# Convolution taps inside the first projection, per-token norm sums, and a tail shared with GpSimd

## The reference, cut to what matters

```python
def conformer_conv(h, w_pw1, b_pw1, w_dw, b_dw, ln_g, ln_b, w_pw2, b_pw2):
    u = h @ w_pw1 + b_pw1                      # 512x1024 @ 1024x2048
    a, gate = jnp.split(u, 2, axis=-1)
    u = a * jax.nn.sigmoid(gate)
    u = lax.conv_general_dilated(              # causal, depthwise, 31 taps
        u, w_dw[:, None, :], window_strides=(1,), padding=[(CONV_WIDTH - 1, 0)],
        dimension_numbers=("NWC", "WIO", "NWC"), feature_group_count=CONV_CHANNELS) + b_dw
    u = jax.nn.silu(layernorm(u, ln_g, ln_b))  # mean and variance over the 1024 channels
    return u @ w_pw2 + b_pw2

def dilated_group(q, k, v, bias_table, window, dilation): ...
    bias = jnp.transpose(bias_table[t5_bucket(dist * dilation)], (2, 0, 1))   # a diagonal of the table per head
    logits = jnp.einsum("bnidhc,bnjdhc->bndhij", qb, kk) * (HEAD_DIM ** -0.5) + bias

def second_block(x, ...):
    ...
    h = h + rms_norm(mixed, mix_norm_post[l])  # MIX_POST in the kernel
    hn = rms_norm(h, ffn_norm_pre[l])          # FFN_PRE
    ...
    return h + rms_norm(ffn, ffn_norm_post[l]) # FFN_POST
```

## Time and profile before

| what | value |
|---|---|
| median of three runs | 1901.59 us |
| the profiled execution's own time | 1901.71 us |
| its span | 1899.9 us |
| mean granted PE clock | 0.971 |
| PE, DVE, ACT, POOL busy | 93%, 57%, 35%, 12% of the span |
| share of the chain that ended last: PE, DVE, ACT | 77%, 17%, 3% |

### The profile page before, as it was taken

How to read it: one execution, slowest core, us unless ns; L and a number is a source line. 1 busy time by engine, 2 the same in 40 slices (tenths; PEclk the granted TensorE clock), 3 DMA queues, 4 the chain that set the end, 5 groups by cost and what they waited for, 6 DMA issues and landing times.

```text
span 1899.9 us, 20795 instructions
## 1 busy us (share of the span) xinstructions
PE 1775.3 (93%) x7977; PEld 1394.9 (73%) x7977; DVE 1088.5 (57%) x1277; ACT 666.1 (35%) x951; POOL 222.3 (12%) x136
## 2 busy tenths in 40 slices
PE   6969699999999999999999999989899699999996
PEld 5747388888888878778888888756456478888884
DVE  6999755442444555664424444568646777626754
ACT  4234343221223244332212234555443344314431
POOL 2013210000000200010000013661200300000001
PEclk9979899999999999999999999989998899999998
DMA  4212012331232311122312322422201112322221
GB/s 178 87 44 73 1 67 89 115 117 67 88 120 91 118 67 56 68 102 107 121 67 91 116 92 100 144 73 80 68 37 67 66 67 88 124 87 88 97 92 44
DMA packets 29151, 164.54 MB, mean 87 GB/s; under 512 B 4347, under 2 KB 7035, under 8 KB 12700
## 3 DMA queue, kind: packets, MB, share of 16 engines
q1 hardware_dynamic: 24800, 158.11, 23.6%
q10 hardware_dynamic: 4284, 5.53, 0.9%
HBM read 153.92 MB, written 4.46 MB: 83 GB/s over the span
## 4 chain that ended last, share of the span: by engine, by line
PE 77%; DVE 17%; ACT 3%; issue 2%; POOL 1%; DMA 0%; ACTq 0%; DVEq 0%; SPq 0%; POOLq 0%
PE PS L592 24%; PE PS L594 24%; PE PS L593 24%; DVE CV L1662 3%; DVE T_hid L1662 3%; DVE W_lo L1632 2%; DVE R L1617 1%; DVE H_lo L1612 1%; ACT W_hi L1036 1%; DVE X L2186 1%; DVE SSUM L2075 1%; PE PS L934 1%; PE PS L886 1%; DVE CV L1675 1%; POOL ISC L1583 1%
## 5 line engine op out<-in xcount | busy, mean ns | idle before, releaser
L592 PE MATMUL PS<-H_hi,W_hi 128*128 128x512 f32 x1600 | 645.6, 403 | 42.7 <-DVE W_lo L1632 22.2
L593 PE MATMUL PS<-H_lo,W_hi 128*128 128x512 f32 x1600 | 628.7, 393 | 0.0
L594 PE MATMUL PS<-H_hi,W_lo 128*128 128x512 f32 x1600 | 628.7, 393 | 0.0
L1036 ACT ACTIVATE W_hi<-W_raw 128x2048 fp32r<-128x2048 f32 (+2 forms) x132 | 266.6, 2020 | 761.6 <-PE PS L594 761.5
L592 PEld LDWEIGHTS PS<-H_hi,W_hi 128*128 128x128 f32 x1600 | 303.8, 190 | 131.1 <-issue 56.7
L1632 DVE TENSOR_TENSOR W_lo<-W_raw,W_hi 128x2048 fp32r<-128x2048 f32 (+2 forms) x132 | 335.6, 2542 | 45.4 <-ACT W_hi L1036 45.1
L594 PEld LDWEIGHTS PS<-H_hi,W_lo 128*128 128x128 f32 x1600 | 303.6, 190 | 65.1
L593 PEld LDWEIGHTS PS<-H_lo,W_hi 128*128 128x128 f32 x1600 | 304.1, 190 | 60.3 <-issue 1.9
L592 PE MATMUL PS<-HID_hi,W_hi 128*128 128x512 f32 x640 | 250.7, 392 | 10.0 <-DVE HID_lo L1738 9.9
L1499 POOL TENSOR_TENSOR SSUM<-SSUM,SQ 128x512 f32<-128x512 f32 x52 | 93.6, 1799 | 1378.4 <-ACT SQ L1069 1375.8
L593 PE MATMUL PS<-HID_lo,W_hi 128*128 128x512 f32 x640 | 250.0, 391 | 0.0
(11 more groups left out here) (263 smaller groups left out, 1460.2 us busy)
## 6 DMA issues: line engine op xcount, KB each, us to landing
W_raw<-in_inp SPq DMA_DIRECT2D x13, 1024.0 KB, 4.8
W_raw<-in_pw SPq DMA_DIRECT2D x12, 1024.0 KB, 4.8
W_raw<-in_gu0a SPq DMA_DIRECT2D x11, 1024.0 KB, 4.7
W_raw<-in_gu0b SPq DMA_DIRECT2D x11, 1024.0 KB, 4.8
W_raw<-in_gu1a SPq DMA_DIRECT2D x11, 1024.0 KB, 4.8
W_raw<-in_gu1b SPq DMA_DIRECT2D x11, 1024.0 KB, 4.7
W_raw<-in_gu2a SPq DMA_DIRECT2D x11, 1024.0 KB, 4.7
W_raw<-in_gu2b SPq DMA_DIRECT2D x11, 1024.0 KB, 4.8
```

The costliest lines, as they stand in the source:

```text
L592: nc.tensor.matmul(dst[:], wh, x_hi[:, k, :], start=(k == first), stop=False)
L593: nc.tensor.matmul(dst[:], wh, x_lo[:, k, :], start=False, stop=False)
L594: return nc.tensor.matmul(dst[:], wl, x_hi[:, k, :], start=False, stop=(k == last))
L1036: nc.scalar.activation(W_hi[b][:, 0:n], W_raw[b][:, 0:n], ACT.Copy).then_inc(w_hi, 1)
```

## The change

- **Taps inside pw1.** PE does 105 taps (tiles 1 and 3 whole, tile 5 from tap 7, tile 7 from tap 12). One tap's three products (L703 to L705 of the new code) follow each k-tile's three from pw1's unit 3 on: 80 taps there and 25 behind. DVE does 143 taps. ACT makes all the diagonals, hi and lo, twelve of 128x128 for each chunk of six taps, in three buffers. POOL makes none.
- **Bias table.** Three products after the last tap, one per group of four heads, leave 4x384 values in PSUM. ACT copies them to fvec, now 4x3x384 and in the memory of H_hi. Three DMAs, each read from four partitions with a broadcast of 128, write the same bias_scratch. ACT waits for all three ahead of the first feed-forward's first H_hi; DVE's wait is gone.
- **LayerNorm.** The sums of squares are column products (one column of ones; one token per partition, 128x4 in all). The root and the reciprocal are of 128x4. Four products with a broadcast and the identity spread the result back over a PSUM bank (`token_spread`). Two small activations load ACT's tables early. The last weight split of pw1 on DVE stands behind the mean's subtractions.
- **MIX_POST, FFN_POST.** The same column sums (`token_sum`) and spreads. ACT's squares stand ahead of its weight splits, and the last unit's splits (ACT's and DVE's) stand behind the root and behind the first two tiles.
- **Tail.** For FFN_POST, DVE does tiles 0 to 4 and writes its temporary to PSUM. ACT scales Y of tiles 5 to 7 and copies R, and POOL multiplies and adds. The output DMAs are issued in another order.
- In pw1's unit 0 ACT's root for the first norm stands ahead of the weight split.

```diff
+PE_TILES = [(1, 0), (3, 0), (5, 7), (7, 12)]
+DVE_TILES = [(0, 31), (2, 31), (4, 31), (5, 7), (6, 31), (7, 12)]
+DVE_TAPS = [5, 8, 21, 24, 24, 24, 24]
+CHUNK = 6
+FIRST_TAP = 48
...
+            def token_sum(n):
...
+                    for b in range(4):
+                        last = nc.tensor.matmul(AUX[0][:, b:b + 1], tokens(src, b), ones[:, 0:1],
+                                                start=(part == 0 and b == 0), stop=(part == 2 and b == 3))
+            def token_spread(bank, made):
+                for b in range(4):
+                    last = nc.tensor.matmul(tokens(bank, b), R4[:, b:b + 1].to_broadcast([P, P]), ident, start=True, stop=True)
...
-                    nc.tensor.matmul(AUX[1 + h % 2][:, 0:DIAG], table_wide[:, h, :], onehot[:, h // GROUP_HEADS, :],
-                                     start=True, stop=True).then_inc(fvec_ps, 1)
+                for g in range(3):
+                    nc.tensor.matmul(PS[1 + g][0:GROUP_HEADS, 0:DIAG], table[:, GROUP_HEADS * g:GROUP_HEADS * (g + 1)],
+                                     onehot[:, g, :], start=True, stop=True).then_inc(fvec_ps, 1)
...
+                        last = product(j % 2, L.kt, half, k, H_hi, H_lo)
...
+                        n = SLOTS * j + 8 * half + k - FIRST_TAP
+                        if n >= 0:
+                            conv_tap(n)
...
+                if n == FFN0 and m.i is None and m.c == 0:
+                    act.wait_ge(scr_out, 48)
...
-            act.dma_start(bias_scratch.rearrange("h p d -> p h d"), fvec[:]).then_inc(scr_out, 16)
+            for g in range(3):
+                act.dma_start(bias_scratch[GROUP_HEADS * g:GROUP_HEADS * (g + 1)],
+                              fvec[:, g, :].unsqueeze(1).to_broadcast([GROUP_HEADS, P, DIAG])).then_inc(scr_out, 16)
...
-            dve.wait_ge(scr_out, 16)
...
+            for n in range(POOL_LAST):
+                m = DT - POOL_LAST + n
+                pool.wait_ge(y_scaled, n + 1)
+                nc.gpsimd.tensor_tensor(Y[:, m, :], Y[:, m, :], R[:], ALU.mult).then_inc(t_pool, 1)
+                pool.wait_ge(t_pool, n + 1)
+                nc.gpsimd.tensor_tensor(X[:, m, :], X[:, m, :], Y[:, m, :], ALU.add).then_inc(x_pool, 1)
```

More of the change, by code:

```diff
@@ L275, in build @@
         CVacc = T_hid
[L277 to L281, removed]
+        UP_hi = sb("UP_hi", [P, 2, PADDED], F32R, at=arena + 17408)
+        UP_lo = sb("UP_lo", [P, 2, PADDED], F32R, at=arena + 21760)
+        D_hi = [sb(f"D_hi{i}", [P, CHUNK, P], F32R, at=w_at + 11264 * i + 8192) for i in range(3)]
+        D_lo = [sb(f"D_lo{i}", [P, CHUNK, P], F32R, at=w_at + 11264 * (3 + i) + 8192) for i in range(3)]
         tap_hi = sb("tap_hi", [P, CONV_WIDTH * DT], F32R, at=arena + 68352)
@@ L663, in _ @@
[L663 to L688, removed]
-            last = nc.tensor.matmul(AUX[3][:], ones, CV[:, CONV_DVE - 1, :], start=False, stop=True)
-            last.then_inc(ln_sum_ready, 1)
+                pe.wait_ge(tab_in, 32)
@@ new lines, in _ @@
+            L = layers["pw1"]
+            unit(L, At(0), H_hi, H_lo, after(h_lo_made, 0))
+            rms_sum(0)
+            for j in range(1, L.n):
+                pe.wait_ge(w_lo, j + 1)
+                if j >= 2:
+                    pe.wait_ge(acc_free, j - 1)
+                for half in range(2):
+                    for k in range(L.kt):
+                        last = product(j % 2, L.kt, half, k, H_hi, H_lo)
+                        if k == L.kt - 1:
+                            last.then_inc(acc_ready, 1)
+                        n = SLOTS * j + 8 * half + k - FIRST_TAP
+                        if n >= 0:
+                            conv_tap(n)
@@ L1140, in _ @@
-            steps(act, L.n, glu_step, first=1, last=2)
-            conv_hi(2)
-            act.wait_ge(fvec_made, 12)
-            act.dma_start(bias_scratch.rearrange("h p d -> p h d"), fvec[:]).then_inc(scr_out, 16)
-            for n, (m, t0, t1) in enumerate(CONV_CHUNKS):
-                if n:
-                    diagonal_hi(n)
-                if n == 0:
-                    split_hi(act, L, At(L.n - 1))
-                if t0 and m > CONV_DVE:
-                    take_conv(m - 1)
-            take_conv(DT - 1)
+                nc.scalar.activation(UP_hi[:, p % 2, 0:n], U[:, m, 0:n], ACT.Copy).then_inc(u_hi, 1)
@@ new lines, in diagonals @@
+            def diagonals(c):
+                if c == 0:
+                    act.wait_ge(w_parts, 2)
+                if c >= 3:
+                    act.wait_ge(conv_pe, CHUNK * (c - 2))
+                for x, (m, t) in enumerate(PE_TAPS[CHUNK * c:CHUNK * (c + 1)]):
+                    for dst, tap in ((D_hi, tap_hi), (D_lo, tap_lo)):
+                        w = tap[:, t * DT + m:t * DT + m + 1].bitcast(F32)
+                        last = nc.scalar.activation(dst[c % 3][:, x, :], ident, ACT.Copy, scale=w)
+                last.then_inc(diag_made, 1)
@@ new lines, in take_bias, with warm_table @@
+            def take_bias(g):
+                act.wait_ge(fvec_ps, g + 1)
+                nc.scalar.activation(fvec[:, g, :], PS[1 + g][0:GROUP_HEADS, 0:DIAG], ACT.Copy).then_inc(fvec_made, 1)
+            def warm_table(function, n):
+                if n:
+                    act.wait_ge(warmed, n)
+                nc.scalar.activation(warm[:, 0:1], epst[:], function).then_inc(warmed, 1)
+            for g in range(SLOTS, SLOTS * L.n):
+                beside_pw1(g)
+            glu_gate(L.n - 1)
@@ L1643, in _ @@
             HALO = CONV_WIDTH - 1
-            todo = [(m, t) for m in range(CONV_DVE) for t in range(CONV_WIDTH if m < CONV_DVE - 1 else CONV_SPLIT)]
+            todo = [(m, t) for m, end in DVE_TILES for t in range(end)]
+            taken_steps = [0]
             def conv(count, upto):
```

350 lines of the change are left out of this document (210 added, 140 removed).

## The result

The changed kernel takes 1926.99 us (median of 4 runs, 1924.4 to 1928.94), the kernel before 1901.24 in the same comparison: a ratio of 1.0132, 95% interval 1.0115 to 1.0150. It is slower by 25.7 us where I forecast 8.5.

The account below looks back on a forecast made before the run. PE was taken to bound most of the time, with taps' and LayerNorm's gains hidden beneath the table's DMA. Sum: 1901.7 + 19.0 (DMA stall) - 7.2 (MIX_POST) - 3.3 (tail) = 1910.2 us; range 1853 to 1917.

Parts of the forecast that it names:

- Taps: pw1 and convolution: last tap ends at 179.4, last join at 182.1, 29.7 us earlier; DVE barely keeps up.
- Rate of the table's DMA: Bias table: one partition group yields 29 GB/s, so the DMAs take 83 us and land at 270; chance 0.72.
- My two engines at 141 ns a packet: Bias table: two engines serve a partition group, each 2048-byte packet taking 141 ns, giving 29 GB/s.
- Who waits: Feed-forward's start: ACT's first H_hi waits for the table until 270, making the layer 19.0 us later than before.
- Everywhere else PE is the bound, and the change leaves that alone: Outside the changed places: PE bounds the time and nothing moves; no term in the sum.
- no rival: DMA no bound: 1858.1, chance 0.20 (0.17 near 1858); late taps beside the stall: up to 1917.7, chance 0.05.
- LayerNorm: From last join to first scaling: 14.2 us instead of 17.5, scaling at 196.3; the gain lies beneath the DMA.
- my 8.5 us for subtracting and squaring with PE cold: Part of LayerNorm's 14.2 us: subtracting and squaring, with the table load ahead and PE cold, take 8.5.
- MIX_POST: Norm after the mixer: R ready 9.4 us earlier, 7.2 net of DVE's deferred split; bounds 5 and 9.4.
- the deferred split of 2.29 us: MIX_POST: DVE's deferred weight split stands between the first tiles, cutting the gain from 9.4 to 7.2 us.
- Tail: Kernel's end: POOL ends last at 1894.1 against 1897.39, -3.3 us; -4.6 if its instructions take 1.3 us each.

Follow-up runs that it names:

- x_spread: The changed kernel with the table's four source rows on partitions 0, 8, 16 and 24 instead of 0 to 3: 1884.92 us, ratio 0.9918 to before.
- x_nowait: The changed kernel with fvec in other memory and no wait ahead of the feed-forward's first H_hi: 1912.82 us, ratio 1.0063 to before.
- b_arena: The kernel before with HID's region 128 bytes higher, nothing else changed: 1910.40 us, ratio 1.0056.
- x_best: The changed kernel with the table read from 128 partitions, HID at its old address, and the table's DMAs issued behind LayerNorm's squares: 1860.99 us.
- x_tail0: x_best with the tail on DVE alone, POOL having no tile: 1862.74 us.
- x_tail2: x_best with POOL doing only tiles 6 and 7 of the tail and DVE six: 1860.62 us, ratio 0.9790 to before.
- x_wide: The changed kernel with the bias table's three DMAs reading from all 128 partitions instead of four: 1875.20 us, ratio 0.9867 to before.
- x_lnfull: x_best with LayerNorm's variance by full sums, root and reciprocal of 128x512, as before the change: 1858.14 us, ratio 0.9776 to before.
- x_final: x_lnfull with POOL doing two tiles of the tail instead of three: 1858.73 us, ratio 0.9779 to before.
- b_plus384: The kernel before with HID's region 384 bytes higher: 1911.27 us, one run.

## Why the prediction was wrong

The direction was right, and so was the table's DMA as the term that decides. The size was not. Two steps failed: what I costed at nothing outside the changed places, and where ACT waits. The first is most of the miss. LayerNorm's part had the wrong sign, which the stall hid.

- **Taps.** Right. The last tap ended at 179.7 (forecast 179.4) and the last join at 182.7 (182.1). DVE just kept up; once it stood 3.3 us for a sigmoid behind a chunk of diagonals, and PE never waited.
- **Rate of the table's DMA.** The limit of the group was right, the term mis-sized. I chose 83 us; the copies in the earlier trace rows had given 29 GB/s by my working, this source gives 25.4. The first H_hi started at 276.9, not 270: +25.7 us at split 16 where I had +19.0. x_spread shows the shared path by its packets. My two engines at 141 ns a packet were not what came: 3.5 engines took 210 ns, for smaller packets. It was partly luck that the product of the two came out so near. The Trainium skill ("SBUF — State Buffer", "Door 1: The DMA port swizzle") has 27.6 GB/s for partitions 0 to 3, closer than my rows but still above what this trace shows.
- **Who waits.** This step failed. I had ACT issue three DMAs at 182.3 and go on, to stop at H_hi. It stopped in the issues themselves, for 40.7 us. In the changed kernel both end in the same landing, so the sum hardly shows it; x_nowait does. Taking the wait away, as my working would have advised, leaves a kernel that is 12 us slower than before. I had counted what is queued behind the wait, but not behind an issue.
- **What I costed at nothing by not looking.** "Everywhere else PE is the bound, and the change leaves that alone" failed: the diff moves the start of HID by 128 bytes, and each down projection of 264 products takes 1.75 us longer, +11.1 us in all with the attention's output projection. b_arena is that edit alone, +9.7. This is the largest part of the miss, and no rival covered it. The mixer, -1.1 us without any change to its code, was at nothing in my sum too; its cause stays open.
- **LayerNorm.** Wrong in sign. I had the new form take 14.2 us from the join to the first scaling, 3.3 less than the 17.5 before. x_best takes 19.0, x_tail0 18.9, x_tail2 20.0, and x_wide 20.9 with its issues in the way: 1.4 us or more lost, not 3.3 won. With full sums x_lnfull takes 16.1 and x_final 18.4, the difference between the two being the sums' clock and the table's issues, not the code. So the column form costs something here, between 0.5 and 4 us by these executions, 2.9 and 1.9 by the medians of the two like pairs (1860.99 to 1858.14, 1860.62 to 1858.73). Whether the table loaded early and the split moved gain anything, no run took apart. The mis-sized term is my 8.5 us for subtracting and squaring with PE cold: the column sums alone took 12.4. In the changed kernel the DMA hid all of it.
- **MIX_POST.** Mis-sized: -8.6 for -7.2. R came 8.7 us earlier against PE's last product, where I had 9.4: from the last square to the root the column sums took 1.2 us and not 0.6. But the deferred split of 2.29 us, which I had taken off, cost nothing: DVE did it behind the first tile's H_lo, and PE started at once (1530.15) without waiting for it.
- **Tail.** -4.4 for -3.3; POOL's instructions took 1.27 us each, its pitch 1.3.

Against the forecast's 8.5 the profiled execution has + 6.7 (landing) + 11.1 (address) - 1.1 (mixer) - 1.4 (MIX_POST) - 1.1 (tail) = 22.7, as measured. The runs' median lies 2.6 us above that execution.

## What to carry to other kernels

Look at how many partitions a transfer reads, not only at its bytes: spreading the source over all partitions cost one small copy and turned 92 us into some 7. Count a DMA's issue as work of the engine that issues it, with everything queued behind it, whenever a former DMA on its queue is slow. And when a change allocates anything, compare the addresses of all the tiles behind it, even those whose code is the same. Before you put a difference of 2 us between two executions down to an edit, look at the granted clock in both, and at the stages that the edit left alone.

## What I had not expected of the hardware

- Three DMAs of 512 rows each, on ACT's queue: the second and the third issue held the engine 9.4 and 30.5 us at 25 GB/s, while one DMA of 1536 rows before took 0.41 us to issue. Each of these two issues went through when some 370 rows of the DMAs before it were left to send (145 of 512 rows sent at 192.5, 653 of 1024 at 223.0). In x_wide, with 15 engines busy, the third issue was through with 694 rows left. Whether a single DMA out of four partitions would hold ACT wasn't tried.
- While the table went out, SP's load of a weight unit took 16.9 us instead of 4.8. That the two share engines is the likely reason, not a shown one; nobody waited for it.
- Products that read HID 128 bytes (modulo 256) from where it stood against the other tiles: 87 in 20 us instead of 90, in b_arena, b_plus384 and the changed kernel alike.
- The 16 passes of the tail's spread took 2.05 us in the changed kernel and 3.78 in x_best and x_tail0, at the same place in the program; the granted clock was 0.50 there. PE had done the same work just before in all three, and in x_tail2, x_lnfull and x_final, which took 2.05. So a tail has 1.7 us that the code doesn't decide, as much as the differences between the tails that I compared.
